# A hybrid decoder step on one core: ScalarE writes the second copy of a head's first turned queries, and the attention stage's pieces and turns stand in other slots

## What is computed

```python
def fox_prompt(q, k, v, logf):               # 8 heads of 64, 2048 rows
    c = cumsum(logf)
    s = (q_i . k_j) * 64 ** -0.5 + c_i - c_j  # where j <= i, else -inf
    return softmax(s) @ v
def mem_attention(q_m, mem_k, mem_v):         # 4 heads of 64, 256 memory tokens
    return softmax(q_m . mem_k * 64 ** -0.5) @ mem_v
```

## Time and profile before

| what | value |
|---|---|
| time, median of 3 runs | 2763.81 us (2754.64 to 2765.43) |
| the profiled execution: its own time, its span | 2763.06 us, 2761.3 us |
| mean granted TensorE clock | 0.978 of 2.4 GHz |
| busy: PE, DVE, ACT, POOL | 2629.5, 1943.0, 1163.7, 1705.4 us |
| attention stage | about 539 to 1147 us of the span |
| copies of queries by DMA (L1501) | 32, of 128 KB, median 4.1 us to landing |

### The profile page before, as it was taken

How to read it: one execution, slowest core, us unless ns; L and a number is a source line. 1 busy time by engine, 2 the same in 40 slices (tenths; PEclk the granted TensorE clock), 3 DMA queues, 4 the chain that set the end, 5 groups by cost and what they waited for, 6 DMA issues and landing times. The chain is left out here.

```text
span 2761.3 us, 42301 instructions
## 1 busy us (share of the span) xinstructions
PE 2629.5 (95%) x14729; PEld 2380.6 (86%) x14729; DVE 1943.0 (70%) x2560; ACT 1163.7 (42%) x2012; POOL 1705.4 (62%) x971
## 2 busy tenths in 40 slices
PE   8999999899999999899979998999999999999998
PEld 7999898877777877777879998999989997888887
DVE  5366687488888887676577788778787875445664
ACT  4212321376777778633343333333433332223243
POOL 3476688488999999565556665666666660222232
PEclk9999999999999999899999999999999999999999
DMA  6588898565666677766635433543435546754564
GB/s 210 169 264 249 268 302 291 167 176 164 172 187 175 181 186 190 232 230 200 206 89 160 130 114 114 168 131 115 130 111 130 177 113 195 241 177 168 186 223 140
DMA packets 471365, 499.21 MB, mean 181 GB/s; under 512 B 172123, under 2 KB 359446, under 8 KB 470122
## 3 DMA queue, kind: packets, MB, share of 16 engines
q1 hardware_dynamic: 449730, 469.97, 56.3%
q10 hardware_dynamic: 21136, 25.50, 2.7%
q0 software_dynamic: 288, 1.05, 0.1%
HBM read 398.07 MB, written 94.16 MB: 178 GB/s over the span
## 5 line engine op out<-in xcount | busy, mean ns | idle before, releaser
L2618 PE MATMUL ps_gate_up<-h_hi,w_hi 128*128 128x344 f32 (+1 forms) x1848 | 594.6, 322 | 26.9 <-DVE h_lo L2508 16.0
L2620 PE MATMUL ps_gate_up<-h_hi,w_lo 128*128 128x344 f32 (+1 forms) x1848 | 595.0, 322 | 0.0
L2619 PE MATMUL ps_gate_up<-h_lo,w_hi 128*128 128x344 f32 (+1 forms) x1848 | 594.4, 322 | 0.0
L2618 PEld LDWEIGHTS ps_gate_up<-h_hi,w_hi 128*128 128x128 f32 x1848 | 350.5, 190 | 30.7 <-DVE h_lo L2508 19.0
L2620 PEld LDWEIGHTS ps_gate_up<-h_hi,w_lo 128*128 128x128 f32 x1848 | 351.0, 190 | 0.0
L2619 PEld LDWEIGHTS ps_gate_up<-h_lo,w_hi 128*128 128x128 f32 x1848 | 350.8, 190 | 0.0
L878 PE MATMUL ps_proj<-w_hi,h_hi 128*128 128x428 f32 (+1 forms) x800 | 288.6, 361 | 7.0 <-ACT proj_out L602 6.9
L879 PE MATMUL ps_proj<-w_lo,h_hi 128*128 128x428 f32 (+1 forms) x800 | 284.9, 356 | 0.0
L880 PE MATMUL ps_proj<-w_hi,h_lo 128*128 128x428 f32 (+1 forms) x800 | 284.2, 355 | 0.0
L1600 DVE TENSOR_TENSOR p_lo<-ps_turned,p_hi 128x512 fp32r<-128x512 f32 (+1 forms) x352 | 211.3, 614 | 77.1 <-ACT p_hi L1491 75.4
L2395 POOL TENSOR_TENSOR stock<-common 128x512 f32<-128x512 f32 x65 | 103.5, 1593 | 248.4 <-DVE w_lo L2493 234.4
(11 more groups left out here) (347 smaller groups left out, 6679.4 us busy)
## 6 DMA issues: line engine op xcount, KB each, us to landing
stock<-in_cache_k SPq DMA_DIRECT2D x192, 256.0 KB, 3.4
common<-in_cache_v SPq DMA_DIRECT2D x172, 256.0 KB, 3.1
stock<-act_combined SPq DMA_DIRECT2D x56, 704.0 KB, 4.2
common<-in_w_gate SPq DMA_DIRECT2D x33, 1024.0 KB, 6.4
common<-in_w_up SPq DMA_DIRECT2D x33, 1024.0 KB, 5.7
common<-in_w_down SPq DMA_DIRECT2D x44, 512.0 KB, 6.0
page_v<-in_cache_v SPq DMA_DIRECT2D x84, 256.0 KB, 3.1
common<-in_w_in SPq DMA_DIRECT2D x44, 428.0 KB, 4.8
```

The costliest lines, as they stand in the source:

```text
L2618: pe.matmul(acc, a_hi, h_hi[:, m, d, 0:n], start=d == 0, stop=False)
L2619: pe.matmul(acc, a_hi, h_lo[:, m, d, 0:n], start=False, stop=False)
L2620: mm = pe.matmul(acc, a_lo, h_hi[:, m, d, 0:n], start=False, stop=d == H - 1)
```

## The change

A turn's first quarter (`j == 0`) is no longer copied by a DMA: ScalarE writes it to the lower half of `q_hi` with a second instruction from the same PSUM bank, and raises `in_hi` only after this one. The pieces of rows 0 to 3 then wait for `in_lo` alone. The other three quarters keep their DMA. Beside it the tables of slots and the order of items in the opening, in the lead to the memory heads and inside the memory heads are changed. The last item of the opening moves from slot 11 to slot 10, so the opening is 14 slots, not 15.

```diff
-THIRD_AT = (0, 1, 3, 3, 3, 4, 5, 7, 8, 8, 10, 14)
-START_AT = (1, 1, 2, 4, 4, 4, 6, 7, 8, 9, 10, 11)
-MEMORY_LEAD_AT = (0, 1, 2, 4, 4, 5, 7, 8, 11, 13)
-MEMORY_AT = (0, 0, 1, 2, 3, 3, 4, 5, 6, 8)
+THIRD_AT = (1, 1, 2, 3, 3, 4, 5, 7, 8, 8, 10, 14)
+START_AT = (1, 2, 4, 4, 4, 4, 7, 8, 9, 9, 10, 10)
+MEMORY_LEAD_AT = (1, 2, 2, 3, 4, 5, 6, 7, 11, 13)
+MEMORY_AT = (0, 1, 1, 2, 3, 4, 4, 5, 6, 8)
@@ lead_items, for the first memory head
-    return [Turn(head, "k", 0), Turn(head, "q", 0), Turn(head, "q", 2), Turn(head, "q", 1), pieces[0], SplitV(head), pieces[1], Turn(head, "q", 3), pieces[2], pieces[3]]
+    return [Turn(head, "q", 2), Turn(head, "q", 0), Turn(head, "k", 0), Turn(head, "q", 1), pieces[0], Turn(head, "q", 3), SplitV(head), pieces[1], pieces[2], pieces[3]]
@@ memory_items
-    return [Turn(head, "k", 0), Turn(head, "q", 0), Turn(head, "q", 1), pieces[0], SplitV(head), Turn(head, "q", 2), pieces[1], Turn(head, "q", 3), pieces[2], pieces[3]]
+    return [Turn(head, "k", 0), Turn(head, "q", 0), Turn(head, "q", 1), pieces[0], Turn(head, "q", 2), pieces[1], SplitV(head), Turn(head, "q", 3), pieces[2], pieces[3]]
@@ first_items
-    return [Turn(0, "kq", 0), Turn(0, "kq", 1)] + fox_pieces(0, range(2)) + [SplitV(0)] + fox_pieces(0, range(2, 6)) + [Turn(0, "kq", 2)] + fox_pieces(0, range(6, 8))
+    return [Turn(0, "kq", 0), Turn(0, "kq", 1)] + fox_pieces(0, range(0, 3)) + [SplitV(0)] + fox_pieces(0, range(3, 5)) + [Turn(0, "kq", 2)] + fox_pieces(0, range(5, 8))
@@ score, on TensorE
-                    if is_fox(item.head):
-                        pe.wait_ge(q_copied[item.rows[-1] // 4], 16 * (item.head + 1))
+                    if is_fox(item.head) and item.rows[-1] >= QCH:
+                        pe.wait_ge(q_copied[item.rows[-1] // QCH - 1], 16 * (item.head + 1))
@@ the turn, on ScalarE
                                 act.activation(a.k_st[0:HD, cols], src[0:HD], ACT.Copy).then_inc(s.k_hi, 1)
+                                if item.j == 0:
+                                    act.activation(a.q_hi[HD:P, cols], src[HD:P], ACT.Copy, scale=SCALE)
+                                    act.activation(a.q_hi[0:HD, cols], src[HD:P], ACT.Copy, scale=SCALE).then_inc(s.in_hi, 1)
+                                    continue
                                 act.activation(a.q_hi[HD:P, cols], src[HD:P], ACT.Copy, scale=SCALE).then_inc(s.in_hi, 1)
                                 act.wait_ge(s.in_hi, turn_index[item] + 1)
-                                act.dma_start(a.q_hi[0:HD, cols].bitcast(F32), a.q_hi[HD:P, cols].bitcast(F32)).then_inc(q_copied[item.j], 16)
+                                act.dma_start(a.q_hi[0:HD, cols].bitcast(F32), a.q_hi[HD:P, cols].bitcast(F32)).then_inc(q_copied[item.j - 1], 16)
```

More of the change, by code:

```diff
@@ L956 @@
 SECOND_AT = (0, 1, 2, 3, 4, 5, 7, 7)
-THIRD_AT = (0, 1, 3, 3, 3, 4, 5, 7, 8, 8, 10, 14)
-START_AT = (1, 1, 2, 4, 4, 4, 6, 7, 8, 9, 10, 11)
-MEMORY_LEAD_AT = (0, 1, 2, 4, 4, 5, 7, 8, 11, 13)
-MEMORY_AT = (0, 0, 1, 2, 3, 3, 4, 5, 6, 8)
+THIRD_AT = (1, 1, 2, 3, 3, 4, 5, 7, 8, 8, 10, 14)
+START_AT = (1, 2, 4, 4, 4, 4, 7, 8, 9, 9, 10, 10)
+MEMORY_LEAD_AT = (1, 2, 2, 3, 4, 5, 6, 7, 11, 13)
+MEMORY_AT = (0, 1, 1, 2, 3, 4, 4, 5, 6, 8)
 def lead_items(head):
     if is_fox(head):
-        return ([Turn(head, "kq", 0), Turn(head, "kq", 1)] + fox_pieces(head, range(2)) + [SplitV(head)] +
-                fox_pieces(head, range(2, 5)) + [Turn(head, "kq", 2)] + fox_pieces(head, range(5, 8)))
+        return ([Turn(head, "kq", 0), Turn(head, "kq", 1)] + fox_pieces(head, range(0, 2)) + [SplitV(head)] + fox_pieces(head, range(2, 5)) +
+                [Turn(head, "kq", 2)] + fox_pieces(head, range(5, 8)))
     pieces = [Piece(head, tuple(range(QCH * ch, QCH * ch + QCH)), 0, MEM, True) for ch in range(NT // QCH)]
-    return [Turn(head, "k", 0), Turn(head, "q", 0), Turn(head, "q", 2), Turn(head, "q", 1), pieces[0], SplitV(head), pieces[1], Turn(head, "q", 3), pieces[2], pieces[3]]
+    return [Turn(head, "q", 2), Turn(head, "q", 0), Turn(head, "k", 0), Turn(head, "q", 1), pieces[0], Turn(head, "q", 3), SplitV(head), pieces[1], pieces[2], pieces[3]]
 def memory_items(head):
     pieces = [Piece(head, tuple(range(QCH * ch, QCH * ch + QCH)), 0, MEM, True) for ch in range(NT // QCH)]
-    return [Turn(head, "k", 0), Turn(head, "q", 0), Turn(head, "q", 1), pieces[0], SplitV(head), Turn(head, "q", 2), pieces[1], Turn(head, "q", 3), pieces[2], pieces[3]]
+    return [Turn(head, "k", 0), Turn(head, "q", 0), Turn(head, "q", 1), pieces[0], Turn(head, "q", 2), pieces[1], SplitV(head), Turn(head, "q", 3), pieces[2], pieces[3]]
 def first_items():
-    return [Turn(0, "kq", 0), Turn(0, "kq", 1)] + fox_pieces(0, range(2)) + [SplitV(0)] + fox_pieces(0, range(2, 6)) + [Turn(0, "kq", 2)] + fox_pieces(0, range(6, 8))
+    return [Turn(0, "kq", 0), Turn(0, "kq", 1)] + fox_pieces(0, range(0, 3)) + [SplitV(0)] + fox_pieces(0, range(3, 5)) + [Turn(0, "kq", 2)] + fox_pieces(0, range(5, 8))
 def at_slots(slots, items):
@@ L1136, in attend @@
         ps_o = psum("ps_out", [P, BLK])
-        names = ("row_summed low_zeroed in_turned q_copied0 q_copied1 q_copied2 q_copied3 k_hi in_hi in_lo turned t_hi t_lo pv scored min made probs v_hi v_lo o_copied o_ready inverted o_out row_made row_out "
+        names = ("row_summed low_zeroed in_turned q_copied1 q_copied2 q_copied3 k_hi in_hi in_lo turned t_hi t_lo pv scored min made probs v_hi v_lo o_copied o_ready inverted o_out row_made row_out "
                  "q0 q1 k0 k1 v0 v1 decay page0 page1 page2 weighed halved added st0 st1 st2 st3 row_st0 row_st1 "
@@ L1142, in attend @@
             conv_in = (s.conv_in0, s.conv_in1)
-            q_copied = (s.q_copied0, s.q_copied1, s.q_copied2, s.q_copied3)
+            q_copied = (s.q_copied1, s.q_copied2, s.q_copied3)
             page_in, stored, row_stored = (s.page0, s.page1, s.page2), (s.st0, s.st1, s.st2, s.st3), (s.row_st0, s.row_st1)
```

## The result

The changed kernel takes 2741.9 us by the median of ten runs (2736.7 to 2747.0), the kernel before 2759.6 by the median of ten (2751.7 to 2765.4). The ratio is 0.994, with a 95% interval of 0.9927 to 0.9954: 16.6 us less by the ratio, where 11.0 were forecast. The three runs shown ahead of the prediction are among the ten, and their median lies 4 us higher. 0.994 of that median is 2747.2, so about half of the miss (5.3 us) is the baseline and the other half (5.6 us) the gain.

The account below looks back on a forecast made before the run. The prediction took GpSimd's chain, following TensorE's pace up to page group 55, to bound the attention stage. 1.9 + 7 x 1.3 = 11.0 us off 2763.06 gave about 2752.1, plus 0.75 for the runs' median: 2752.8 us, range 2744 to 2763.

Parts of the forecast that it names:

- The bound: Attention stage, 603 us: GpSimd's chain ends it, following TensorE's pace to page group 55; TensorE's lead there is the gain.
- The end of the stage is not TensorE's: End of the attention stage: GpSimd's chain ends it, with TensorE's own last store just before it.
- worth at most what TensorE and GpSimd stand idle: Attention stage: the gain is limited to the idle time of TensorE, 52 us, and GpSimd, 45 us.
- I take 1.3 us a head: Third phase of seven fox heads: earlier first score, partly lost at unit 6; 1.3 us each, bounds 0 and 2.9.
- more than that: Rival, chance 0.27: shorter stalls leave the clock up, each head gives nearly 2.9 us; about 16 us gained, 2747.
- The opening: Opening of the attention stage: reordered pieces close VectorE's gaps; gain 1.9 us, bounds 0.5 and 3.5.
- The pages: SyncE's page loads, a slot later against the units: some groups move behind waits, GpSimd's idle time swallows it; cost 0.
- The second copy: ScalarE's added 592 ns instruction, eight times: replaces the DMA's wait and issue, so costs ScalarE nothing; `q_lo` comes 0.6 us later.
- The memory heads: Memory heads, after page group 55: TensorE may gain up to 1 us a head, three times; worth 0 to the stage.
- The stall only moves: Rival, chance 0.21: VectorE limits, unit 6's wait takes all the heads' gain; 0 to 6 us remain, 2760.
- The sum: Whole kernel: 1.9 + 7 x 1.3 = 11.0 us gained, forecast 2752.8 us.

Follow-up runs that it names:

- e12: The kernel before, with GpSimd's second addition per page group on 512 elements instead of 1024: ratio 0.9991 to the kernel before.
- e4: The kernel before, with 20 products of constants on TensorE ahead of the first score's waits in heads 1 to 7: ratio 0.9973 to the kernel before.
- e7: The changed kernel with a third ScalarE instruction before the signal, writing the bank's values back in place: ratio 0.9945 to the kernel before.
- e3: The changed kernel with the copy and the third phase's new slots, but opening and memory heads as before: ratio 0.9962 to the kernel before.
- e6: The changed kernel with every page load and sample row one slot earlier: ratio 0.9946 to the kernel before.
- e5: The changed kernel with the memory heads' tables and orders of before: ratio 0.9939 to the kernel before.
- e11: The changed kernel with GpSimd's second addition per page group on 512 elements instead of 1024: ratio 0.9917 to the kernel before.

## Why the prediction was wrong, point by point

**The bound** was read rightly in what the sum needs: the gain is TensorE's lead, passed on by the pages to group 55, and 17.0 of 17.1 us are there at group 55. Two sentences of it went too far. "The end of the stage is not TensorE's" is not borne out, since a GpSimd with 60 us less to do shortened the kernel before by nothing that can be told from noise (e12). And "worth at most what TensorE and GpSimd stand idle" holds busy time fixed, while TensorE's fell by 12 us at the higher clock.

**The step that failed: "I take 1.3 us a head", the term 7 x 1.3 = 9.1 us.** TensorE gained 442.6 - 427.8 = 14.8 us over the seven phases, 2.1 each. The 1.3 held the shorter stalls alone, minus the new wait, and priced the clock at nothing, though the rows of before showed it at 0.81 and 0.62 and the text had worked out 1.7 us for one head. e4 shows the clock's share with nothing moved: 1.2 us each. The remaining 0.9 are by subtraction the stalls, less than the 1.3 forecast. The splits do not carry the gain: the seven took 18.1 us before, 18.0 in e4 and 19.7 after. The reason for leaving the clock out was that stalls of 1.3 and 1 us would remain; with stalls of 1.05 us before the first score (1.49 in head 5) and 0 to 2.5 before unit 6 the clock stayed at 1.00 in all seven. That was a near thing (e7). The case that came true is the rival "more than that", at 0.27, with its reason. That its size fits as well, 16 us forecast and 16.6 measured, is in part luck: it took 22 us of lead and lost 6 of them in the pages, where 18.1 were measured and 1 was lost.

**The opening: 1.9 us forecast.** At the mark that the forecast used, the first `p_hi`, 4.0 us are measured (23.3 and 19.3), above the upper bound of 3.5; at head 0's third phase 3.3 are left, and 3.3 is also the mean difference at the first `p_hi` between the seven kernels with the old opening and the seven with the new. The missing 1.4 us are the split of the values. It took 3.83 us before and 2.67 after, and this was not the chance that the prediction called it: with the old opening it takes 3.3 to 4.1 us in all seven kernels, with the new one 2.1 to 2.7. GpSimd's first instruction starts 8.3 us after the stage's start before and 6.9 after, the split 9.2 and 9.0, so the split finds 2.75 us of that instruction left before and 1.6 after. In the seven later heads the place is chance, and their splits came out no shorter in the mean.

**The pages: "Cost 0".** Right for the groups that were feared: no wait stands before group 29. Short in one respect: the text let "most of the 6.49 us before group 11 go" and gave it no worth, since GpSimd was ready for TensorE's 11 us anyway. That is true for 11 us. With a lead of 18.1 us at head 7 (3.3 and 14.8) it decides: from group 11 to 55 GpSimd has 9 us of idle time to give, and in e3, where group 11 waits as before, 13.2 us of TensorE's gain became 10.1. In the changed kernel group 11 starts 9.0 us earlier, because the opening is a slot shorter and sample row 0's store no longer stands before the next head's loads. That the slot is a cause is shown by e6 in the profile, for 5.2 of the 9.0 us, and not by the times.

**The second copy, 0**: 593 ns, eight times, and and TensorE's largest wait for ScalarE, for the probabilities, is 5.6 us in sum before and after. Its 0.6 us lie in the 1.05 us of wait for `q_lo`, as forecast. Right. **The memory heads, 0**: right within what the times tell (e5).

**"The stall only moves" (0.21)** did not come. Its wait is there in head 2, 1.24 us for `p_lo`, at the place and nearly the size forecast, and of the 3.0 us by which head 2's first score comes earlier 1.7 are left at unit 6. VectorE is busy for 8.45 of 9 us behind head 2's start, against 7.54 before, and would be the next limit there.

**The sum**, with the measured terms, is 3.3 + 14.8 = 18.1 us of TensorE's lead, of which the stage kept 17.1 and the times 16.6 by the ratio. What stays open is how the last 6 us between e3 and the changed kernel divide among the opening, group 11 and the memory heads: the profiles give 2 to 4 us to each, and the intervals of the two kernels touch.

## What to carry to other kernels

A stall of TensorE has two prices, the wait and the work done at 1.2 GHz behind it; read both from the granted clock in short windows behind each stall, and put the second in the sum, not in a rival. Useless products in the stall measure it in one experiment. And a lead on one engine is worth what the slower chain beside it has as idle time from its first late input on: before adding up gains per head, look at when that chain starts.

Where an instruction of VectorE has very different lengths from one time to the next, look at what GpSimd is doing when it begins, before calling the length chance: a change of order can move it against GpSimd's instructions for good, as it did in this opening.

The two edits of this change are worth nothing like their sum: slots that expect queries early cost 6 us while the queries come by DMA, and bring some 7 us once ScalarE writes them (0.9967 and 0.994).

## What the runs showed of the hardware that was not expected

- 140 products more made the stage 7.9 us shorter (e4).
- A first score's wait of 1.05 us had a clock of 1.00 behind it each time; 1.53 us had 0.81 to 0.86 behind five of six of them (e7), and one of 1.98 us had 1.00.
- The 128x1024 split of VectorE took 1.22 to 1.27 us where GpSimd's running instruction was at its end or none ran, and otherwise the rest of that instruction plus 1.08 us (98 of 98, up to 4.57 us). A GpSimd instruction that begins beside the split takes 3.42 us instead of 2.4.
- ScalarE's copy from the bank's partitions 64 to 127 into partitions 0 to 63 takes 593 ns, the same as the copy that stays in its partitions.
- 60 us of GpSimd's work could be left out of a stage in which it is busy for 559 of 592 us, and the stage became 0.8 us shorter (e11).
